# Mixer projections in a two-block fp32 kernel: token shift added from PSUM, head norms on 8 rows, decay factor in the exponentials, blocks of a and r side by side

## The reference

```python
h = rms_norm(x, mix_norm[l])
p = h @ w_in[l]
p_rwkv = token_shift(p[..., :SHIFT_COLS], shift_mu[l])      # u + (prev - u) * mu, prev = u one token earlier
p_fox = p[..., SHIFT_COLS:SHIFT_COLS + FOX_COLS]
gates = jax.nn.sigmoid(p[..., SHIFT_COLS + FOX_COLS:])
...
w_log = -jax.nn.softplus(-(w0 + jnp.tanh(w_lo) @ w_up)) - 0.5
decay = jnp.exp(-jnp.exp(w_log))
a = jax.nn.sigmoid(a0 + a_lo @ a_up)
kk = k * k_k
kk = kk / jnp.maximum(jnp.sqrt(jnp.sum(kk * kk, axis=-1, keepdims=True)), 1e-12)   # per head of 64
k = k * (1.0 + (a - 1.0) * k_a)
y = rwkv7_recurrence(r, decay, k, v, -kk, kk * a)
...
x = x + (gate_a * y_a + gate_b * y_b) @ w_out[l]
```

## Time and profile before

| | |
|---|---|
| median of three runs | 2848.49 us (2841.59 to 2848.59) |
| profiled execution | 2840.36 us, span 2838.6 us |
| TensorE busy | 2723.9 us, 96% of the span |
| VectorE busy | 1872.3 us, 66% |
| ScalarE busy | 1262.5 us, 44% |
| GpSimd busy | 737.6 us, 26% |
| mean granted TensorE clock | 0.981 |

### The profile page before, as it was taken

How to read it: one execution, slowest core, us unless ns; L and a number is a source line. 1 busy time by engine, 2 the same in 40 slices (tenths; PEclk the granted TensorE clock), 3 DMA queues, 4 the chain that set the end, 5 groups by cost and what they waited for, 6 DMA issues and landing times.

```text
span 2838.6 us, 43607 instructions
## 1 busy us (share of the span) xinstructions
PE 2723.9 (96%) x17496; PEld 2464.1 (87%) x17496; DVE 1872.3 (66%) x3279; ACT 1262.5 (44%) x1763; POOL 737.6 (26%) x326
## 2 busy tenths in 40 slices
PE   8998999999999998879999999999989999999998
PEld 7888999999788886679999998888879887887997
DVE  5655997777555556657987775555565578656554
ACT  4433455333445544534463334554444465332443
POOL 0000888666000000105996662000000021010000
PEclk9999999999999999989999999999999999999999
DMA  6564555444666664245554445666645553113554
GB/s 202 163 193 149 177 180 163 138 140 141 200 192 192 190 191 128 97 141 158 177 173 140 141 142 178 192 189 192 192 144 183 189 163 125 45 53 100 168 185 157
DMA packets 124282, 451.54 MB, mean 159 GB/s; under 512 B 13856, under 2 KB 13984, under 8 KB 123952
## 3 DMA queue, kind: packets, MB, share of 16 engines
q1 hardware_dynamic: 122256, 441.57, 49.0%
q0 software_dynamic: 1824, 7.17, 0.8%
HBM read 446.59 MB, written 2.10 MB: 158 GB/s over the span
## 4 chain that ended last, share of the span: by engine, by line
PE 90%; DVE 5%; POOL 3%; ACT 1%; issue 1%; DMA 0%; DVEq 0%; SPq 0%; POOLq 0%; ACTq 0%
PE ps L447 13%; PE ps L448 13%; PE ps L449 13%; PE ps L482 11%; PE ps L484 11%; PE ps L483 11%; PE ps L587 4%; PE ps L469 3%; PE ps L470 3%; PE ps L471 3%; DVE W L1427 2%; POOL lo L2206 2%; PE ps L712 2%; DVE x L1427 1%; PE ps L433 1%
## 5 line engine op out<-in xcount | busy, mean ns | idle before, releaser
L994 ACT ACTIVATE hi<-ring 128x1024 fp32r<-128x1024 f32 x830 | 878.4, 1059 | 1187.4 <-PE ps L449 640.0
L2206 POOL TENSOR_TENSOR lo<-ring,hi 128x1024 fp32r<-128x1024 f32 x272 | 689.6, 2541 | 1527.0 <-ACT hi L994 1527.0
L1450 DVE TENSOR_TENSOR lo<-ring,hi 128x1024 fp32r<-128x1024 f32 x558 | 682.8, 1225 | 565.3 <-ACT hi L994 564.5
L447 PE MATMUL ps<-xT_r,hi 128*128 128x256 f32 x3248 | 935.3, 288 | 13.1 <-POOL lo L2206 9.5
L448 PE MATMUL ps<-xT_r,hi 128*128 128x256 f32 x3248 | 920.2, 283 | 0.0
L449 PE MATMUL ps<-xT_r,lo 128*128 128x256 f32 x3248 | 919.8, 283 | 0.0
L447 PEld LDWEIGHTS ps<-xT_r,hi 128*128 128x128 f32 x3248 | 624.4, 192 | 17.2 <-issue 6.4
L448 PEld LDWEIGHTS ps<-xT_r,hi 128*128 128x128 f32 x3248 | 625.0, 192 | 0.8 <-issue 0.7
L449 PEld LDWEIGHTS ps<-xT_r,lo 128*128 128x128 f32 x3248 | 624.3, 192 | 0.0
L482 PE MATMUL ps<-hi,oht_r 128*128 128x512 f32 x1040 | 410.9, 395 | 6.0 <-DVE W L1427 4.6
L484 PE MATMUL ps<-hi,oht_r 128*128 128x512 f32 x1040 | 408.2, 392 | 0.0
(11 more groups left out here) (217 smaller groups left out, 2692.8 us busy)
## 6 DMA issues: line engine op xcount, KB each, us to landing
ring<-in_peer_u SPq DMA_DIRECT2D x256, 512.0 KB, 3.5
ring<-in_peer_v SPq DMA_DIRECT2D x256, 512.0 KB, 4.2
ring<-in_f SPq DMA_DIRECT2D x132, 512.0 KB, 3.5
ring<-in_ret_vg SPq DMA_DIRECT2D x32, 512.0 KB, 3.5
ring<-in_peer_q SPq DMA_DIRECT2D x32, 512.0 KB, 3.6
ring<-in_ret_qk SPq DMA_DIRECT2D x16, 512.0 KB, 4.3
ring<-in_ret_out SPq DMA_DIRECT2D x16, 512.0 KB, 4.1
ring<-in_in_shift SPq DMA_DIRECT2D x14, 512.0 KB, 3.6
```

Source lines behind the costliest of these rows:

```text
L447: pe.matmul(o, h, xT[:, k, 0:256], start=k == 0, stop=False)
L994: hid.done(a.activation(hi[m % NH][:, :], ring[j % NR][:, :], ACT.Copy), j)
L1450: lo_v.done(v.tensor_tensor(lo[m % NH][:, :], ring[j % NR][:, :], as32(hi[m % NH][:, :]), ALU.subtract), j)
L2206: lo_p.done(p.tensor_tensor(lo[m % NH][:, :], ring[j % NR][:, :], as32(hi[m % NH][:, :]), ALU.subtract), j)
```

## The change

Six edits, all in the mixer.

1. Shift: ScalarE writes (1 - mu) times the bank's value straight to its place (two activations of 128x256), and VectorE adds mu times the bank's value one column earlier, read from PSUM (two instructions of 128x255). The buffer with the zero column and the subtraction are gone; VectorE frees the bank, not ScalarE.
2. Head norms: `kk2` now multiplies by a matrix with 8 columns, so that the 8 head sums stand on 8 rows, in one bank. Floor, square root and reciprocal work on 8x256. Four new matmuls with 8 rows (`kk_all`) spread the result over 128 rows after shift 5, and VectorE multiplies k by kk and by that in one instruction a chunk.
3. Keys: ScalarE makes 1 - ka + ka * a, VectorE multiplies it by k in one instruction of 128x1024.
4. Decay: the factor -exp(-0.5) moves from a pass of VectorE into the scale of the three exponentials.
5. Products: the two mask results of a bank stand side by side in one buffer (`M_LB`, `M_MK`), so that one instruction of 128x512 does a bank.
6. At the mixer's start VectorE makes 1 - mu and 1 - ka (14 and 4 columns) and an 8x512 copy of the identity's corner; two small memsets are gone.

```diff
@@ shift, ScalarE and VectorE
-                    act.done(a.activation(M_U[i % 2][:, :, 1:257], j2(ps("shift", i)), ACT.Copy), "shift", i)
-                    empties(act, "shift", i)
+                    for j in range(2):
+                        act.done(a.activation(M_P[:, p0 + j, :], ps("shift", i)[:, j * 256:j * 256 + 256], ACT.Identity,
+                                              scale=pc("omu", p0 + j)), "shift", i)
...
-                    tt_(M_dif, u[:, :, 0:256], u[:, :, 1:257], ALU.subtract)
                     for j in range(2):
-                        stt_(M_P[:, p0 + j, :], M_dif[:, j, :], pc("mu", p0 + j), u[:, j, 1:257], ALU.mult, ALU.add,
-                             name=("shift", i))
+                        own = M_P[:, p0 + j, 1:256]
+                        stt_(own, ps("shift", i)[:, j * 256:j * 256 + 255], pc("mu", p0 + j), own, ALU.mult, ALU.add, name=("shift", i))
+                    empties(dve, "shift", i)
@@ head norms, TensorE
-                head_sums("kk2", M_kn)
-                for i in range(4, 7):
+                b = bank("kk2", among=FX)
+                for c in range(4):
+                    ins = pe.matmul(b[0:8, 0:256], C("hsel")[:, 6 - 2 * c:14 - 2 * c], c4(M_kn)[:, c, :], start=c == 0, stop=c == 3)
+                mm.done(ins, "kk2")
+                for i in range(4, 6):
                     shift(i)
+                pe.wait_ge(*at(dve, "kk_inv"))
+                for c in range(0, 4, 2):
+                    b = bank("kk_all", c, among=FX)
+                    for j in range(2):
+                        o = (c + j) * 128
+                        ins = pe.matmul(b[:, j * 256:j * 256 + 256], M_heads[:, o:o + 128], M_nrm, start=True, stop=True)
+                    mm.done(ins, "kk_all", c)
+                shift(6)
@@ head norms, keys and decay, VectorE (in the places that the rows below show)
-                ts_(M_lgd, M_lgd, -math.exp(-0.5), None, ALU.mult)
-                for c in range(4):
-                    ts_(c4(M_kk)[:, c, :], k_[:, c, :], pc("kk", c), None, ALU.mult)
-                    ts_(c4(M_kn)[:, c:c + 2, :], j2(ps("kk2", c)), 1e-24, None, ALU.max, name=("kk_norm", c))
+                ts_(M_nrm, ps("kk2")[0:8, 0:256], 1e-24, None, ALU.max, name=("kk_norm",))
-                step(v.reciprocal, M_kn[:, 0:512], M_kn[:, 0:512])
+                step(v.reciprocal, M_nrm, M_nrm, name=("kk_inv",))
-                step(v.reciprocal, M_kn[:, 512:1024], M_kn[:, 512:1024])
-                tt_(M_kn, M_kn, M_kk, ALU.mult)
-                keys(0)
-                keys(1)
+                v.wait_ge(*at(act, "ka"))
+                tt_(M_kk, M_tmp, flat(k_), ALU.mult)
-                keys(2)
-                keys(3)
+                for c in range(0, 4, 2):
+                    v.wait_ge(*at(mm, "kk_all", c))
+                    for j in range(2):
+                        stt_(c4(M_kn)[:, c + j, :], k_[:, c + j, :], pc("kk", c + j), ps("kk_all", c)[:, j * 256:j * 256 + 256],
+                             ALU.mult, ALU.mult)
+                    empties(dve, "kk_all", c)
@@ ScalarE
+                for c in range(4):
+                    act.done(a.activation(c4(M_tmp)[:, c, :], c4(M_av)[:, c, :], ACT.Identity, scale=pc("ka", c), bias=pc("oka", c)), "ka")
...
-                act.done(a.activation(M_eP, M_eP, ACT.Exp), "decay_p")
+                act.done(a.activation(M_eP, M_eP, ACT.Exp, scale=DECAY), "decay_p")
...
-                act.done(a.activation(M_kn, M_kn, ACT.Sqrt), "kk_norm")
+                act.done(a.activation(M_nrm, M_nrm, ACT.Sqrt), "kk_norm")
@@ products, VectorE
-                            pv = ps(name, g, half).rearrange("p (u z k n) -> p z u k n", u=2, z=2, k=2)
-                            o = (g * 4 + half * 2) * 128
-                            for z, dst in enumerate(dsts):
-                                mk = M_mkp[:, z * 64:z * 64 + 64].unsqueeze(1).unsqueeze(1).broadcast_to([128, 2, 2, 64])
-                                tt_(dst[:, o:o + 256].rearrange("p (u k n) -> p u k n", u=2, k=2), pv[:, z], mk, ALU.mult, name=("tri", g))
+                            tt_(dst[:, o:o + 512].rearrange("p (u n) -> p u n", u=2), ps(name, g, half).rearrange("p (u n) -> p u n", u=2),
+                                b3(M_mkp[:, 0:256], [128, 2, 256], 1), ALU.mult, name=("tri", g))
```

More of the change, by code:

```diff
@@ L25 @@
 NEG = -1e30
+DECAY = -math.exp(-0.5)
 LAM_INIT = 0.8 - 0.6 * math.exp(-0.3)
@@ L328, in program @@
         a_ = Area(M_base)
-        M_LT, M_MT, M_BT, M_KT, M_X, M_XT = (a_(2048) for _ in range(6))
+        M_LB, M_MK, M_X, M_XT = a_(4096), a_(4096), a_(2048), a_(2048)
         M_CT, M_T1, M_Vs, M_o = (a_(1024) for _ in range(4))
@@ L897, in mixer @@
                             pe.matmul(o, M_aBD[:, i, :], S[:, c, :], start=True, stop=False)
-                        ins = pe.matmul(o, un(M_MT, i), Vu(i), start=n == 0, stop=True)
+                        ins = pe.matmul(o, pair(M_MK, i, 0), Vu(i), start=n == 0, stop=True)
                     mm.done(ins, "R", n)
@@ L922, in mixer @@
                         o = b[:, c * 64:c * 64 + 64]
-                        pe.matmul(o, un(M_BT, i), M_SA[:, c, :], start=True, stop=False)
-                        ins = pe.matmul(o, un(M_KT, i), Vu(i), start=False, stop=n == 0)
+                        pe.matmul(o, pair(M_LB, i, 1), M_SA[:, c, :], start=True, stop=False)
+                        ins = pe.matmul(o, pair(M_MK, i, 1), Vu(i), start=False, stop=n == 0)
                         if n:
@@ L1210, in shifted @@
                 def shifted(i):
+                    p0 = 2 * SHIFT[i]
                     a.wait_ge(*at(mm, "shift", i))
[L1212 to L1216, removed]
-                    act.done(a.activation(M_U[i % 2][:, :, 1:257], j2(ps("shift", i)), ACT.Copy), "shift", i)
-                    empties(act, "shift", i)
+                    a.wait_ge(*at(dve, "one_less"))
+                    for j in range(2):
+                        act.done(a.activation(M_P[:, p0 + j, :], ps("shift", i)[:, j * 256:j * 256 + 256], ACT.Identity,
+                                              scale=pc("omu", p0 + j)), "shift", i)
                 def fox_tile(i):
@@ L1840, in mixer @@
             def mixer():
+                for whole, rest_of, w in (("mu", "omu", 14), ("ka", "oka", 4)):
+                    ts_(col[:, COLS[rest_of]:COLS[rest_of] + w], col[:, COLS[whole]:COLS[whole] + w], -1.0, 1.0, ALU.mult, ALU.add,
+                        name=("one_less",))
+                step(v.tensor_copy, M_heads.rearrange("p (h d) -> p h d", h=8), b3(ident[0:8, 0:8], [8, 8, 64], 2), name=("heads",))
                 rms("mix", M_xs, ffn_added(1))
@@ L1851, in mm4, with mask, of_four, blocks @@
                     return b3(m, [128, 4, 128], 1)
+                def mask(m):
+                    return M_mkp[:, 128 + m * 64:192 + m * 64]
                 def mm8(m):
-                    return b3(M_mkp[:, m * 64:m * 64 + 64], [128, 8, 64], 1)
+                    return b3(mask(m), [128, 8, 64], 1)
+                def of_four(z, g):
+                    return z[:, g * 1024:g * 1024 + 1024].rearrange("p (u z k n) -> p z u k n", u=4, z=2, k=2)[:, 0]
+                def blocks(z):
+                    return z.rearrange("p (u k n) -> p u k n", u=4, k=2)
+                def mm42(m):
+                    return mask(m).unsqueeze(1).unsqueeze(1).broadcast_to([128, 4, 2, 64])
                 def flat(z):
@@ L1916, in mixer @@
                 shift_tile(4, 0)
-                for c in range(0, 4, 2):
-                    v.wait_ge(*at(mm, "kk2", c))
-                    ts_(c4(M_kn)[:, c:c + 2, :], j2(ps("kk2", c)), 1e-24, None, ALU.max, name=("kk_norm", c))
-                    empties(dve, "kk2", c)
+                v.wait_ge(*at(mm, "kk2"))
+                ts_(M_nrm, ps("kk2")[0:8, 0:256], 1e-24, None, ALU.max, name=("kk_norm",))
+                empties(dve, "kk2")
                 shift_tile(4, 1)
@@ L2347, in constants @@
     put("bdones", bd.astype(f))
+    put("hsel", np.stack([(p // 64 == j - 6) & (j in (6, 7)) for j in range(14)], 1).astype(f))
     put("eye2", (p[:, None] % 64 == np.arange(64)[None, :]).astype(f))
@@ L2381, in tables @@
         out.append(lev(t, s, 1 << q))
-    mtab = np.concatenate([(o[:, :64] | o[:, 64:]).astype(f) for o in out], 1)
+    mtab = np.concatenate([(o[:, :64] | o[:, 64:]).astype(f) for o in out[:1] * 2 + out[1:2] * 2 + out[2:]], 1)
     return rtab, mtab
```

39 lines of the change are left out of this document (18 added, 21 removed).

## The result

The change made the kernel slightly slower: 2849.61 us (median of 12 runs, 2846.82 to 2850.63) against 2842.35 for the kernel before (12 runs, 2840.06 to 2850.02). The ratio is 1.002, 95% interval 1.0012 to 1.0028. The profiled execution has a span of 2847.8 us for 2838.6, +9.2. The three runs of the kernel before from which the forecast was counted are among the 12; two of them (2848.49 and 2848.59) lie near the upper end of what it does.

The account below looks back on a forecast made before the run. TensorE, with 90% of the chain that ended last, was taken to bound the kernel. Gains of 5.5 and 0.45 us, summed as 6.0, took 2848.5 to 2842.5 us (profiled execution 2840.4 to 2834.4); range 2834 to 2851.

Parts of the forecast that it names:

- VectorE's sum: Mixer before the first fox tiles: VectorE's instructions and their gaps take 14.6 us less in all.
- the three gaps: TensorE's waits between shift and fox tiles for late low halves of weight tiles: three of four close.
- The fourth gap: Before fox projection 1, TensorE waits for banks that ScalarE empties: 2.6 us, stays as before.
- The spreading matmuls: Four new 8-row matmuls spreading the inverse norms, on TensorE's path in the shift stage: 1.54 us added, bounds 0 and 3.1.
- Place A: Between shift and fox tiles, to fox projection 1: 5.5 us gained, the new matmuls' 1.54 already taken off.
- rival 4: Weak 8-column and 8-row matmuls pull the clock down in the shift stage or rounds: 3.4 us a fall; chance 0.10.
- Place B: End of the last product round, TensorE's 2.66 us wait before the score matmul: 0.45 us gained, bounds 0 and 2.66.
- Rival 1: The clock's fall after the last product round goes too: 3.0 us more, 2839.5; chance 0.25.
- Its addition: Later rounds' clock falls, 2478 to 2502, also go: 3.4 us more, 2836; chance 0.10 within the 0.25.
- "The recurrence, the level steps and everything later keep their instructions": Rest of the mixer and after: instructions unchanged, bank numbers rotate by one with the same releasers, no time counted.
- The starting level: The forecast subtracted its 6.0 us from 2848.5 us, the median of three runs of the kernel before.

Follow-up runs that it names:

- `oht` first: Kernel after with buffer oht allocated ahead of tables con and col, at byte 213120, no instruction changed: 2827.44 us, again 2827.73 us.
- the operand elsewhere: Kernel after, TensorE's loaded operand in the two peer_v stages taken from xT, oht still written, output not the reference's: 2829.78 us, one run.
- 16 words of gap: Kernel before with an unused 64-byte gap right before oht, so only oht moves, to byte 221056: 2832.33 us, ratio 0.9966.

## Why the prediction was wrong

By its steps:

- **VectorE's sum and the three gaps: right.** Reciprocal 1.73 us for 1.67; VectorE is busy for 13.4 us less ahead of the rounds (90.12 - 76.74), for a sum of 14.6 that counts the gaps between instructions too. In the kernel with `oht` first the low halves of fox tiles 0, 2 and 3 are ready 4.4, 1.5 and 0.8 us before they are wanted, forecast 3.4, 1.3 and 0.8. The fourth gap stayed. VectorE's idle time for ScalarE was left out, so the reserve was larger than the sum said.
- **The spreading matmuls: too cheap.** 2354.42 - 2352.29 = 2.13 us, less the 0.12 of a usual step: 2.0 for 1.54. Place A gave 4.85 us (39.44 - 34.59) for 5.5 where the clock held.
- **The clock behind them: rival 4's first fall.** The kernel after has it (windows above), and so has the experiment with the operand elsewhere; it costs 1.5 us (36.09 - 34.59). The five kernels with the edited mixer and `oht` first have none, with the same matmuls there. The first of them:

```profile
2325.37:2329.37 4.00, 4.00 (x26) 3.48 (x26) 3.52 (x5) 2.08 (x4) 0.00 (x0) 1.00 0.87 253
```

  The Trainium skill (TensorE: Matmul & The Clock Gate, "What's actually happening") puts falls down to idleness; this one had no idle time before it. Both operands of the spreading matmuls lie in `oht` too. Why the fall comes with `oht` at 221120 (2 of 2 kernels) and not at 213120 (0 of 5) is open.
- **Place B: right**, 0.46 for 0.45, the wait 2.21 for 2.2, and confirmed by putting the two masks back. Rival 1 did not come: the clock stays at 0.79 there. (Over the same 16.5 us it is 0.90 in four experiments: with 16 words of gap, with one and two reciprocals more, and with two masks a bank. The first and the last have the old wait of 2.66 us, so the shorter wait isn't what raises it.) Its addition, that the falls of the later rounds go (3.4 us), came true in the kernel after (1.00 for 0.86 above), and not in the one with `oht` first (0.86). It came too in the kernels before with `oht` 128 bytes further, so it comes with the place of `oht` and not with the mixer's edits; by what mechanism is open.
- **"The recurrence, the level steps and everything later keep their instructions", with all the rest of the program at nothing: the step that failed.** The statement is true and the conclusion is not. The sum took it that a stage with the same instructions takes the same time, and edit 6's wider tables were costed by three small instructions alone. They moved `oht`, and 3072 matmuls in stages far ahead of the mixer pay 14.7 us, 15.3 with the clock at the first stage's start. The rest of the way to kk2 took 0.8 us more (kk2 starts 16.1 us later in all, 2338.97 for 2322.89). With these terms: 15.3 + 0.8 - 3.35 - 0.46 - 2.9 (the rounds, less place B, which come with `oht`'s place) = +9.4, for +9.2 measured between the profiled executions. None of the rivals had this mechanism.
- **The starting level.** The forecast was counted from 2848.49; in 12 runs the kernel before has 2842.35. That the range of 2834 to 2851 holds the measured 2849.61 is luck: counted from 2842.35 it would end near 2845. The sign was wrong: -6.0 forecast, +7.3 measured.

## What to carry to other kernels

A change that widens any buffer moves all that are laid out behind it: compare buffer addresses before and after, and hold those of TensorE's operands in long dense stages fixed when an edit's worth is measured. When the total doesn't fit, count TensorE's records per equal window over the whole span, the untouched stages first; equal busy time hides a change of pace. And before VectorE's work is given a price, subtract the time that it stands idle for others in the same stretch.

## What the runs showed of the hardware

Matmuls of 512 columns with a newly loaded 128x128 operand each ran at 0.2257, 0.2280 or 0.2324 us, by where in 256 bytes the loaded operand's buffer starts (128, 64 and 192 bytes over a multiple, in this order), at a clock of 1.00 and without a gap. The loads themselves show 188 ns over 800 to 1000 in the kernels before, after, with `oht` first and with the operand elsewhere, and lie beside the matmuls:

```profile
L485 PEld LDWEIGHTS ps<-hi,oht_r 128*128 128x128 f32 x286 | 53.8, 188 | 13.0
```

The Trainium skill (TensorE: Matmul & The Clock Gate, "Step-by-step: what each phase is for") says that loading the next operand takes no read bandwidth from the running matmul. The runs here show that the address of what is loaded changes the pace of what runs, by 3%; whether by the port, a bank or a conflict with the streamed operand they do not show.
